# Expert weights read as four neighbouring rows per partition, in one 16 KB run, in a two-part transformer kernel

## The reference, cut to what matters

```python
def expert_block(args):
    idx, wts, e = args
    xb = x_pad[idx]
    a = _clamped_swiglu(xb @ w_gate[e] + b_gate[e], xb @ w_lin[e] + b_lin[e])
    y = a @ w_down[e] + b_down[e]
    return (y * wts[:, None]).astype(h.dtype)
```

## Time and profile before

| | |
|---|---|
| median of three runs | 2802.96 us (2798.93 to 2804.67) |
| the profiled execution, its own time | 2798.76 us |
| its span, first to last instruction | 2797.1 us |
| PE busy | 2504.2 us (90%) |
| PE weight loads busy | 1662.6 us (59%) |
| DVE busy, ACT busy | 1227.2 us (44%), 858.5 us (31%) |
| moved by DMA | 687.46 MB |

### The profile page before, as it was taken

How to read it: one execution, slowest core, us unless ns; L and a number is a source line. 1 busy time by engine, 2 the same in 40 slices (tenths; PEclk the granted TensorE clock), 3 DMA queues, 4 the chain that set the end, 5 groups by cost and what they waited for, 6 DMA issues and landing times. The chain is left out here.

```text
span 2797.1 us, 34161 instructions
## 1 busy us (share of the span) xinstructions
PE 2504.2 (90%) x12924; PEld 1662.6 (59%) x12925; DVE 1227.2 (44%) x1958; ACT 858.5 (31%) x1384; POOL 43.7 (2%) x61
## 2 busy tenths in 40 slices
PE   4998999899799899989989997799888888888887
PEld 2887988688588789868867886333223222322222
DVE  2754765565465475566454454522112112111212
ACT  3444444444344444444344443101001000000101
POOL 0000000000000000000000002000000000000000
PEclk9999999999899999999999998799999999999999
DMA  5763443575475334366351225699999999999984
GB/s 225 258 209 112 144 131 120 210 253 175 167 250 187 133 126 134 128 233 237 132 174 61 71 89 175 254 410 410 410 410 410 410 410 410 410 410 410 410 333 195
DMA packets 186910, 687.46 MB, mean 246 GB/s; under 512 B 20642, under 2 KB 21922, under 8 KB 185666
## 3 DMA queue, kind: packets, MB, share of 16 engines
q1 hardware_dynamic: 178868, 651.41, 62.4%
q0 software_dynamic: 7488, 29.36, 3.0%
q10 hardware_dynamic: 432, 5.08, 0.4%
HBM read 683.70 MB, written 2.11 MB: 245 GB/s over the span
## 5 line engine op out<-in xcount | busy, mean ns | idle before, releaser
L2148 PE MATMUL ps<-wexp_all_second,con_all_whole 128*64 128x512 f32 x3168 | 708.1, 597 | 70.0 <-DMA wexp_all_second<-in_w_lin 69.7
L2148 PEld LDWEIGHTS ps<-wexp_all_second,con_all_whole 128*64 128x64 f32 x3168 | 219.0, 137 | 516.6 <-issue 380.4
L446 DVE TENSOR_TENSOR lo_first<-raw_first,hi_first 128x1024 fp32r<-128x1024 f32 x264 | 308.6, 1221 | 40.6 <-ACT hi_first L416 40.6
L241 PE MATMUL ps<-hi_first,h_hi_first 128*128 128x512 f32 x704 | 285.0, 405 | 23.1 <-DVE lo_first L446 23.1
L242 PE MATMUL ps<-lo_first,h_hi_first 128*128 128x512 f32 x704 | 280.3, 398 | 0.0
L243 PE MATMUL ps<-hi_first,h_lo_first 128*128 128x512 f32 x704 | 280.1, 398 | 0.0
L416 ACT CAST hi_first<-raw_first 128x1024 fp32r<-128x1024 f32 x264 | 260.6, 1053 | 19.2 <-DMA raw_first<-in_ffn_wgu 19.2
L241 PE MATMUL ps<-h_hi_first,w_hi_first 128*128 128x256 f32 x848 | 248.1, 293 | 3.4 <-DVE w_lo_first L891 3.2
L242 PE MATMUL ps<-h_lo_first,w_hi_first 128*128 128x256 f32 x848 | 239.7, 283 | 0.0
L243 PE MATMUL ps<-h_hi_first,w_lo_first 128*128 128x256 f32 x848 | 239.7, 283 | 0.0
L891 DVE TENSOR_TENSOR w_lo_first<-raw_first,w_hi_first 128x1024 fp32r<-128x1024 f32 x122 | 148.7, 1223 | 158.4 <-ACT w_hi_first L802 157.8
(11 more groups left out here) (430 smaller groups left out, 3484.3 us busy)
## 6 DMA issues: line engine op xcount, KB each, us to landing
wexp_all_second<-in_w_gate SPq DMA_DIRECT2D x64, 2048.0 KB, 23.3
wexp_all_second<-in_w_lin SPq DMA_DIRECT2D x64, 2048.0 KB, 23.9
wexp_all_second<-in_w_down SPq DMA_DIRECT2D x64, 2048.0 KB, 22.1
raw_first<-in_ffn_wgu SPq DMA_DIRECT2D x176, 512.0 KB, 4.8
raw_first<-in_w_mix SPq DMA_DIRECT2D x138, 512.0 KB, 3.3
raw_first<-in_ffn_wd SPq DMA_DIRECT2D x88, 512.0 KB, 5.1
raw_second<-in_w_mix SPq DMA_DIRECT2D x57, 512.0 KB, 3.3
wada_first<-in_w_ada POOLq DMA_DIRECT2D x48, 512.0 KB, 4.7
```

Source lines behind the costliest of these rows:

```text
L241: nc.tensor.matmul(out, w_hi, x_hi, start=start, stop=False, skip_group_check=True)
L446: nc.vector.tensor_tensor(lo[:, slot], raw[:, slot], hi[:, slot].bitcast(F32), ALU.subtract).then_inc(s[f"{kind}_lo"], 1)
L2148: mm = nc.tensor.matmul(dst[side(half), :], lhs(k), B.wexp[2 * "gld".index(kind) + part][:, k % 4, half * HALF:(half + 1) * HALF], start=( ...
```

## The change

A partition now takes four neighbouring rows of a half, rows h*512 + 4*p + k for k = 0 to 3, which are one run of 16 KB in HBM and in the buffer. Row group k of a buffer is then the rows 4p + k, so the turned operands have to hold the columns 4p + k at piece k: both turns read every fourth column instead of 128 neighbouring ones. Everything else stands as it was.

```diff
 def expert_weights(sp, B, I, e, kind, half, sem):
     src = {"g": I["w_gate2"], "l": I["w_lin2"], "d": I["w_down2"]}[kind][e]
-    sp.dma_start(B.wexp[2 * "gld".index(kind) + half],
-                 src.rearrange("(k p) n -> p k n", p=P)[:, 4 * half:4 * half + 4, :]).then_inc(sem, 16)
+    sp.dma_start(B.wexp[2 * "gld".index(kind) + half].rearrange("p k n -> p (k n)"),
+                 src.rearrange("(h p k) n -> h p (k n)", p=P, k=4)[half]).then_inc(sem, 16)
...
-                    mm = nc.tensor.transpose(H[:, k * P:(k + 1) * P], B.xg[:, k * P:(k + 1) * P], con("ident"))
+                    mm = nc.tensor.transpose(H[:, k * P:(k + 1) * P], B.xg[:, k:HALF:4], con("ident"))
...
-                    mm = nc.tensor.transpose(A[:, k * P:(k + 1) * P], B.a[:, k * P:(k + 1) * P], con("ident"))
+                    mm = nc.tensor.transpose(A[:, k * P:(k + 1) * P], B.a[:, k:HALF:4], con("ident"))
```

## The result

The changed kernel takes 2759.85 us (median of four runs, 2758.34 to 2764.53), the kernel before 2803.1 in its four. The ratio is 0.9851, with a 95% interval of 0.9834 to 0.9868: faster by 41.8 us (37.0 to 46.5). The forecast was 2765.7 in a range of 2755 to 2782.

A forecast was written before the change was run, and what follows sets the result against it. Weight loads at a flat 410 GB/s were taken to bound the expert stage, 30.72 us a block against PE's 27.59. Loads save 38.3, turns cost 1.0: 2802.96 - 37.3 = 2765.7 us, range 2755 to 2782.

The forecast's parts named there:

- The chain: Expert stage: 174 unbroken loads, from expert 1's d loads to PE's last wait (l1 of expert 30); each load's saving counts 174 times.
- second account, from PE's side: Expert blocks: 28 periods shorter by 1.32 us are 37.0, plus some 1.3 from expert 2's lin half before the first wait.
- The price of a descriptor: Expert weight loads: each descriptor merged away saves 9.1 ns; 24 fewer an engine make 5.12 into 4.90 us, 38.3 us in all.
- The upper bound, 46.1: Expert weight loads: if 16 KB went at 432 GB/s, a load would take 4.855 us, saving 174 x 0.265 = 46.1 us.
- The turns: PE's transposes reading columns four apart: 50 ns more each, 20 unhidden after the last wait, 1.0 us (0 to 3.6).
- SP's queue: Issuing two loads takes 3.8 us with room, 8.7 when full; both under 10.24 us, so shorter issue brings nothing.
- Dear turns: Strided stationary loads make PE bind; break-even 0.317 us a turn; at 0.4 the kernel takes 2824 us; chance 0.06.
- Slower long runs: 16 KB pieces read slower from HBM: at 0.66 us each, a load takes 5.28 us, the kernel 2831 us; chance 0.03.
- A third of the price: Only one third of the rate difference goes with the descriptor: 0.073 us a load, kernel time 2791 us; chance 0.06.
- No change by cutting: Queue cuts 16 KB pieces into 4 KB packets, or 410 GB/s is the ceiling anyway: kernel time 2804 us; chance 0.05.
- The estimate of 3 cycles a packet: Expert weight loads: by the skill page at 850 MHz, 24 fewer descriptors save 85 ns a load, the whole 15 us.

## Why the prediction was right, point by point

**What binds, and how often it counts.** The chain was as told: no hole in the stream from the d load of expert 1 to l1 of expert 30. 174 x (5.120 - 4.894) = 39.3 us; from the issue of that d load to the end of the last wait the trace has 895.13 us before and 855.63 after, 39.5 less. That is 174 loads of 5.120 or of 4.894 and 4.2 or 4.1 us more, so the count holds at both ends.

The prediction's second account, from PE's side, was wrong: 28 periods shorter by 1.32 us and 1.3 more gave the same 38.3 by luck. In the kernel before, the four periods from block 0 to block 4 take 27.59 each, one takes 30.45 and only 25 take 30.72; in the changed kernel 23 are left, at 29.365. These 23 gain 31.2 us. Three more periods, to blocks 5, 6 and 7, gain 8.6 together, since they hardly wait any more. The slower first product and the dearer turns take back 1.1, which makes the 38.7 of the stage. PE's first stop for lin weights, before and after:
```profile
1933.12 3.65 PE L2148 MATMUL ps<-wexp_all_second,con_all_whole 128*64 128x512 f32 x16 [0.96 <-DMA wexp_all_second<-in_w_lin]
```
```profile
2020.28 3.65 PE L2149 MATMUL ps<-wexp_all_second,con_all_whole 128*64 128x512 f32 x16 [1.24 <-DMA wexp_all_second<-in_w_lin]
```
They stand in blocks 5 and 8, three blocks apart where some two were forecast. A faster load does two things in this loop: it shortens the blocks that wait, and it puts off the first wait, since the lead that the loads have over PE at the start of the stage is used up more slowly. The count of loads in the chain covers both.

**The price of a descriptor.** 9.1 ns was read off the load of x. Five lengths of run were measured, each as a sixth of a waiting block, the mean of at least 17 blocks:

| run | descriptors an engine, 2 MB | load, us | step |
|---|---|---|---|
| 2 KB | 64 | 5.421 | |
| 4 KB | 32 | 5.120 | 0.301 / 32 = 9.4 ns |
| 8 KB | 16 | 4.971 | 0.149 / 16 = 9.3 ns |
| 16 KB | 8 | 4.894 | 0.077 / 8 = 9.6 ns |
| 32 KB | 4 | 4.857 | 0.037 / 4 = 9.3 ns |

By this line a load is 4.82 us of bytes (435 GB/s) and 9.4 ns for each descriptor of an engine. Where on the way of a descriptor these 9.4 ns arise, no run shows. 38.3 us were forecast for this part and 39.3 came. The 422 GB/s of the earlier trace rows is what the 8 KB runs then gave; the term was 3% too small mostly because 4 KB were taken at 410 GB/s, 159.8 ns, where 5.120 us for 32 descriptors is 160.0. That it came so close was luck: a window of 2 us with 103 packets fixes its rate to about 1%, 3 ns of the 310.6, and so a third of the 9.1. The upper bound, 46.1, took the 432 GB/s of the earlier trace rows for what 16 KB could reach; the line puts 432 at 32 KB.

**The turns.** This term had the wrong size and the wrong arithmetic. The single stationary load became dearer than assumed, from a median of 140 to one of 212 ns, so 72 and not 50; the period grew by 0.09 us, not by eight times 72 ns. Two things swallow the rest. The loads of a group of four run beside the matmuls of the turn before, and the group took 0.75 instead of 0.66 us. And of the two groups in a block, the second waited for ACT's copy in any case. PE's stationary loads in one block, before, then after:
```profile
2714.87 0.42 PEld L2198 LDWEIGHTS ps<-con_all_whole,sq_whole 128*128 128x128 f32 x4 [0.81 <-issue]
2715.64 0.42 PEld L2134 LDWEIGHTS ps<-con_all_whole 128*128 128x128 f32 x4 [0.35 <-ACT con_all_whole L2238]
```
```profile
2674.93 0.56 PEld L2199 LDWEIGHTS ps<-con_all_whole,sq_whole 128*128 128x128 f32 x4 [0.81 <-issue]
2675.70 0.56 PEld L2135 LDWEIGHTS ps<-con_all_whole 128*128 128x128 f32 x4 [0.20 <-ACT con_all_whole L2239]
```
The wait shrank from 0.35 to 0.20 us by what the first group had taken more. So 1.0 us was forecast behind the last wait and 0.28 came.

**The sum.** 37.3 us were forecast, and by the measured terms 39.3 - 0.28 = 39.0 belong to the change. The stage got 38.66 shorter, since the first down product ran 0.56 us longer in the profiled execution. The median came out 5.9 us under the forecast of 2765.7: 1.7 are the two terms, and for the other 4 there is only the scatter ahead of the stage to point to.

**SP's queue.** The reading of the earlier trace rows was wrong, without harm. The 3.8 us of a row with two loads are not the time to issue them: SP waits in it for PE to free the second half. A single issue shows it, in the view by line of the changed kernel (ns min/median/max):
```profile
L2062 SPq DMA_DIRECT2D wexp_all_second<-in_w_gate x64: 332/336/432, 1732.2 to 2690.7; - x64
L2062 SPq DMA_DIRECT2D wexp_all_second<-in_w_lin x64: 332/333/736, 1733.0 to 2697.7; - x64
```
and the row with two loads still reads 3.8 us. Before, the gate's line had a median of 3832 ns and a minimum of 373. So the issue of 512 descriptors takes 0.37 us at its shortest; what took microseconds later in the stage was, by all signs, a full queue. With a quarter of the descriptors no issue took longer than 0.74 us.

Could the blocked issues themselves have slowed the loads? The runs between speak against it: with 8 KB runs the issues are short already (a median of 373 to 377 ns), and with 2 KB and 4 KB runs they are long (medians of 3.3 to 5.2 us), yet all lie on one line of 9.3 to 9.6 ns a descriptor. The issue was not on the path.

**The rivals.** Dear turns: the stationary loads became 72 ns dearer and the period 0.011 us a turn, against a break-even of 0.317. The rule of the Trainium skill, "SBUF — State Buffer", "Door 1: The DMA port swizzle (why [64,N] ≈ [32,N])", that a read pays when each element stands in another line of 16 bytes, was right about there being a price; the trace makes it 1.5 times on the stationary load, most of it hidden. Slower long runs: none; the rate rose at each doubling up to 32 KB. A third of the price: excluded, all of the 9.1 ns goes with the descriptor. No change by cutting: one run was one packet.

The estimate of 3 cycles a packet (the Trainium skill, "DMA: Bandwidth & Descriptors", "Why small descriptors are slow (HBM only)") would have given 15 us. At 850 MHz, that page's figure, the measured 9.4 ns are 8 cycles.

## What to carry to other kernels

Where a profile shows a long stretch at a flat rate with the DMA engines full, count descriptors, not loads: here each cost an engine about 9.4 ns on top of its bytes, so 2 KB runs lose 11% to it, 4 KB runs 6%, 16 KB runs 1.5%. Let a partition take neighbouring rows of a matrix and permute the other operand to match; the permutation costs nearly nothing if it can ride on a turn that is there anyway. What it brings is the price times the loads in the unbroken stream: from the last one whose start compute sets (here the d load of expert 1) to the last one that compute waits for. Find these two in the trace first.

## What the runs showed of the hardware that was not expected

The price of a descriptor is the same from 2 KB to 32 KB to within 0.2 ns, as far as the spacing of the blocks fixes it, and does not depend on whether the next one reads the bytes behind it or bytes 512 KB away (5.120 us a load in both).

A stationary load of 128 x 128 float32 takes 140 ns from neighbouring columns and about 210 from columns two or four apart. Two apart are 8 bytes, two elements to a line of 16, the case for which the section "Door 1: The DMA port swizzle (why [64,N] ≈ [32,N])" of the Trainium skill's "SBUF — State Buffer" gives the full rate. In the kernel with 8 KB runs, 1900 to 2600 us, it was no cheaper:
```profile
L2135 PEld LDWEIGHTS ps<-con_all_whole 128*128 128x128 f32 x92 | 12.8, 208 | 4.9 <-ACT con_all_whole L2239 4.9
L2199 PEld LDWEIGHTS ps<-con_all_whole,sq_whole 128*128 128x128 f32 x92 | 12.7, 207 | 18.7 <-issue 18.7
```
So here the measurement decides against the rule: a step of two columns costs as much as one of four, though it touches half as many lines. Other steps were not run.
